# NSA score products in two single-pass fp32r matmuls, with a new order of the attention steps

## What is computed

```
kb   = rope(k_slc), kwin = rope(k_win)                 # (512, 2 groups, 64)
s    = einsum('q h d, k d -> h q k', qg, k) * scale     # 4 heads share a group's keys
p    = masked_softmax(s, key <= query)
o    = g_cmp * o_cmp + g_slc * (p_slc @ v_slc) + g_win * (p_win @ v_win)
```

## Time and profile before

| | |
|---|---|
| median of 3 runs | 1097.6 us (1094.86 to 1098.27) |
| the profiled execution | 1095.02 us, its span 1093.2 us |
| granted TensorE clock, mean | 0.996 |
| PE busy | 1073.5 us, 98% of the span |
| PE weight loads | 888.5 us, 81% |
| DVE, ACT, POOL busy | 608.3, 474.4, 481.4 us (56%, 43%, 44%) |
| DMA | 100.10 MB |
| NSA steps | from 754.3 us to about 963 us of the span |

### The profile page before, as it was taken

The page is one execution under the profiler, slowest core; times in us unless marked ns, Lnnn a source line. Parts: engine busy times, 40 slices in busy tenths (PEclk is TensorE's granted clock), DMA queues, the critical chain, the costliest instruction groups (busy, mean ns, idle before and its releaser), DMA issues. The chain is left out here.

```text
span 1093.2 us, 16412 instructions
## 1 busy us (share of the span) xinstructions
PE 1073.5 (98%) x5755; PEld 888.5 (81%) x5755; DVE 608.3 (56%) x1349; ACT 474.4 (43%) x1009; POOL 481.4 (44%) x276
## 2 busy tenths in 40 slices
PE   7999999999999999999999999999999999989996
PEld 6888888888888888888888888887788888767775
DVE  6667746766737556522122125436956765554667
ACT  6644356665543431431331233353334444454545
POOL 5785423232326775774675475356222122113230
PEclk9999999999999999999999999999999999999999
DMA  7554532211106354343442644604112012000011
GB/s 222 139 133 104 132 98 65 59 57 54 40 20 184 95 173 146 104 155 127 133 155 75 180 132 118 154 20 116 40 40 68 20 40 58 20 11 15 20 63 78
DMA packets 167158, 100.10 MB, mean 92 GB/s; under 512 B 30424, under 2 KB 160812, under 8 KB 166060
## 3 DMA queue, kind: packets, MB, share of 16 engines
q1 hardware_dynamic: 166924, 99.06, 31.4%
q10 hardware_dynamic: 160, 0.07, 0.0%
HBM read 95.69 MB, written 3.16 MB: 90 GB/s over the span
## 5 line engine op out<-in xcount | busy, mean ns | idle before, releaser
L1245 POOL TENSOR_TENSOR wlo<-stage,whi 128x1024 fp32r<-128x1024 f32 (+1 forms) x105 | 272.8, 2603 | 216.8 <-ACT whi L741 216.6
L2245 PE MATMUL ps<-hhi,whi 128*128 128x512 f32 (+1 forms) x728 | 311.8, 428 | 2.4 <-DVE gated L2007 1.9
L2245 PE MATMUL ps<-hhi,wlo 128*128 128x512 f32 (+1 forms) x728 | 294.3, 404 | 0.0
L2245 PE MATMUL ps<-hlo,whi 128*128 128x512 f32 (+1 forms) x728 | 285.4, 396 | 0.0
L2245 PEld LDWEIGHTS ps<-hhi,whi 128*128 128x128 f32 (+1 forms) x728 | 137.1, 188 | 37.1 <-issue 6.8
L741 ACT ACTIVATE whi<-stage 128x1024 fp32r<-128x1024 f32 x104 | 109.6, 1055 | 120.5 <-PE ps L2245 89.9
L2245 PEld LDWEIGHTS ps<-hhi,wlo 128*128 128x128 f32 (+1 forms) x728 | 137.3, 189 | 30.1 <-issue 6.3
L1343 POOL TENSOR_TENSOR wlo<-stage,whi 128x1024 fp32r<-128x1024 f32 (+3 forms) x40 | 73.4, 1837 | 190.9 <-ACT whi L1035 190.9
L2245 PEld LDWEIGHTS ps<-hlo,whi 128*128 128x128 f32 (+1 forms) x728 | 137.3, 189 | 24.2
L1123 ACT ACTIVATE prob<-ps,aneg 128x128 f32<-128x128 f32 (+1 forms) x96 | 50.7, 529 | 171.7 <-DVE aneg L2038 121.3
L2245 PE MATMUL ps<-ahi,whi 128*128 128x512 f32 x312 | 124.2, 398 | 0.0
(11 more groups left out here) (401 smaller groups left out, 1770.0 us busy)
## 6 DMA issues: line engine op xcount, KB each, us to landing
stage<-dn_w_in SPq DMA_DIRECT2D x32, 512.0 KB, 4.1
stage<-mlp_w_up SPq DMA_DIRECT2D x32, 512.0 KB, 4.9
stage<-mlp_w_down SPq DMA_DIRECT2D x32, 512.0 KB, 4.6
mod_w<-ada_w SPq DMA_DIRECT2D x8, 1536.0 KB, 6.5
stage<-w_in SPq DMA_DIRECT2D x17, 512.0 KB, 3.6
gcrow<-gc_rows SPq DMA_DIRECT2D x16, 256.0 KB, 3.5
stage<-dn_w_out SPq DMA_DIRECT2D x8, 512.0 KB, 3.7
stage<-w_in SPq DMA_DIRECT2D x9, 256.0 KB, 3.1
```

The source lines that it names most:

```text
L1245: pool.tensor_tensor(wlo[:, slot, 0:ks, 0:cols], stage[:, slot, 0:ks, 0:cols], whi[:, slot, 0:ks, 0:cols], ALU.subtract).then_inc(s["w_lo" ...
L2245: mm = pe.matmul(bank, w[:, slot, k - ks[0], 0:width], x[:, k], start=(i == 0), stop=(i == len(todo) - 1))
```

## The change

For each branch, the keys of one group are split in a high half (fp32r) and a low half (the rest). `kst[b][:, g]` holds the high half on the group's own 64 partitions, and the low half on the other 64. For each pair of steps a query tile is split too: `q_high` has the high half of one head's queries on both halves of the partitions, `q_low[g]` the low half on the group's partitions and zeros on the others. The score is then two fp32r matmuls into one bank: `q_high` by `kst` (high by high and high by low), `q_low` by `kst` (low by high). ACT writes the high halves (4 activations of 64x512 for the keys, 2 of 64x128 for each of 32 query tiles), and DVE the low ones (4 subtractions of 64x512, 32 of 64x128). Where the keys were rotated by two sums of 64x512, one of 128x512 does it, into scratch tiles. POOL zeroes two `q_low` buffers of 128x256 in place of two `kz` of 128x1024.

The order of the NSA steps becomes head, group, query tile, branch: both branches of a query tile follow each other, and share its split. The tile of steps i + 2 and i + 3 is split in step i, at ACT behind `turned(i - 2)`, at DVE as the first of `jobs(i)`. The MLA steps and all sums behind the scores stay. (Hunks with only a new semaphore name or an empty line are left out.)

```diff
@@ -249,7 +249,7 @@
         kT2_at = place[0]
-        kz = [sb("kz0", [P, 2, T]), None]
+        kst = [sb("kst0", [P, 2, T], F32R), None]
         v2 = [sb(f"v2_{b}", [P, CH, P]) for b in range(2)]
@@ -282,7 +282,8 @@
         gated = sb("gated", [P, 2, T])
-        kz[1] = at("kz1", [P, 2, T], F32, gated_at)
+        kst[1] = at("kst1", [P, 2, T], F32R, gated_at)
+        krot = [zth, prob[:, 1]]
         rcos = sb("rcos", [P, T])
@@ -308,7 +309,9 @@
         o_mla = at("o_mla", [P, CH, QW], F32, kT2_at)
-        csq = at("csq", [P, 3, T], F32, mlp_end + 5 * T * 4)
+        csq = at("csq", [P, 3, T], F32, mlp_end + T * 4)
+        q_low = [at(f"q_low{g}", [P, 2, P], F32R, mlp_end + (6 * T + g * 3 * P * 2) * 4) for g in range(2)]
+        q_high = at("q_high", [P, 2, P], F32R, mlp_end + 7 * T * 4)
 
@@ -477,11 +480,15 @@
             if i < N_NSA:
-                return "nsa", i // 16, i // 8 % 2, i // 4 % 2, i % 4
+                return "nsa", i // 16, i % 2, i // 8 % 2, i // 2 % 4
             return "mla", (i - N_NSA) // 4, None, None, i % 4
...
             return slice(g * DK, (g + 1) * DK)
+
+        def query_tile(n):
+
+            return n // 8, n // 4 % 2, n % 4
 
@@ -1085,15 +1092,33 @@
 
+            def key_high(b):
+                after(act, "dve", f"post {('ks', 'kw')[b]}")
+                for g in range(2):
+                    act.activation(kst[b][group(g), g], krot[b][group(g), :], ACT.Copy).then_inc(s["k_hi"], 1)
+
+            def query_high(n):
+                e, g, qt = query_tile(n)
+                after(act, "dve", f"post q{e}")
+                if n >= 2:
+                    act.wait_ge(s["at_s"], 2 * n - 2)
+                src = q2T[group(g), e, qt * P:(qt + 1) * P]
+                act.activation(q_high[group(g), n % 2], src, ACT.Copy)
+                act.activation(q_high[group(1 - g), n % 2], src, ACT.Copy).then_inc(s["qt_hi"], 1)
+
             taken("vs")
...
                 split_two(ahead_of(name))
+                if name == "gk":
+                    key_high(0)
                 if name == "kw":
...
                     done(act.activation(gate2[:, :, :], gate2[:, :, :], ACT.Tanh, scale=0.5), "gate tanh")
+                    query_high(0)
+            key_high(1)
 
@@ -1124,7 +1149,7 @@
             def turned(i):
-                keys = (i % 4 + 1) * P
+                keys = (step_key(i)[4] + 1) * P
                 act.wait_ge(s["at_t"], i + 1)
@@ -1198,6 +1223,8 @@
                     turned(i - 2)
+                if i % 2 == 0 and i + 2 < N_NSA:
+                    query_high(i // 2 + 1)
                 jobs(i)
@@ -1354,9 +1381,7 @@
             pool.memset(o_nsa[:, :, :], 0.0)
-            pool.memset(kz[1][:, :, :], 0.0)
-            pool.memset(minus_half[:, :], -0.5)
-            done(pool.memset(kz[0][:, :, :], 0.0), "zero")
+            done(pool.memset(minus_half[:, :], -0.5), "zero")
 
@@ -1371,12 +1396,16 @@
             for name in UNITS2[0:6]:
...
                     cosine("kr")
+                    after(pool, "dve", "norm low 6")
+                    pool.memset(q_low[0][:, :, :].bitcast(F32), 0.0).then_inc(s["qt_zero"], 1)
+                    pool.memset(q_low[1][:, :, :].bitcast(F32), 0.0).then_inc(s["qt_zero"], 1)
 
@@ -1876,9 +1905,7 @@
                     after(dve, "pool", "zero")
-                    for g in range(2):
-                        ins = dve.tensor_tensor(dst[group(g), g], rcos[group(g), :], rsin[group(g), :], ALU.add)
-                    done(ins, f"post {name}")
+                    done(dve.tensor_tensor(dst, rcos[:, :], rsin[:, :], ALU.add), f"post {name}")
                 else:
@@ -1886,8 +1913,20 @@
 
+            def key_low(b, g):
+                dve.wait_ge(s["k_hi"], 2 * b + g + 1)
+                dve.tensor_tensor(kst[b][group(1 - g), g], krot[b][group(g), :], kst[b][group(g), g], ALU.subtract).then_inc(s["k_lo"], 1)
+
+            def query_low(n):
+                e, g, qt = query_tile(n)
+                dve.wait_ge(s["qt_hi"], n + 1)
+                if n == 0:
+                    dve.wait_ge(s["qt_zero"], 2)
+                dve.tensor_tensor(q_low[g][group(g), n % 2], q2T[group(g), e, qt * P:(qt + 1) * P],
+                                  q_high[group(g), n % 2], ALU.subtract).then_inc(s["qt_lo"], 1)
+
             turned_rows(0, "vs")
-            rotated("ks", kz[0], None)
+            rotated("ks", krot[0][:, :], None)
             rotated("q0", q2T[:, 0], "ks")
@@ -1895,7 +1934,11 @@
             done(dve.tensor_scalar(gate2[:, :, :], gate2[:, :, :], 0.5, 0.5, ALU.mult, ALU.add), "gates")
-            rotated("kw", kz[1], "kr")
+            key_low(0, 0)
+            key_low(0, 1)
+            rotated("kw", krot[1][:, :], "kr")
+            query_low(0)
+            key_low(1, 0)
 
@@ -2025,7 +2068,7 @@
             def most(i):
-                qt = i % 4
+                qt = step_key(i)[4]
                 dve.wait_ge(s["at_s"], i + 1)
@@ -2072,8 +2115,11 @@
             def jobs(i):
+                if i % 2 == 0 and i + 2 < N_NSA:
+                    query_low(i // 2 + 1)
                 if i == 0:
                     turned_rows(1, "vw")
+                    key_low(1, 1)
                 if 3 <= i < 11:
@@ -3002,20 +3048,25 @@
                 if kind == "nsa":
-                    if qt == 0 and g == 0:
-                        after(pe, "dve", f"post {('ks', 'kw')[b]}")
-                        after(pe, "dve", f"post q{e}")
-                    q, k = q2T[:, e, qt * P:(qt + 1) * P], kz[b][:, g, 0:(qt + 1) * P]
+                    n = i // 2
+                    if e == 0 and qt == 0:
+                        pe.wait_ge(s["k_lo"], 2 * b + g + 1)
+                    if b == 0:
+                        pe.wait_ge(s["qt_hi"], n + 1)
+                        pe.wait_ge(s["qt_lo"], n + 1)
+                    keys = kst[b][:, g, 0:(qt + 1) * P]
+                    pe.matmul(bank[:, 0:(qt + 1) * P], q_high[:, n % 2], keys, start=True, stop=False)
+                    pe.matmul(bank[:, 0:(qt + 1) * P], q_low[g][:, n % 2], keys, start=False, stop=True).then_inc(s["at_s"], 1)
                 else:
...
                     q, k = qm[:, e % 4, qt * P:(qt + 1) * P], km[:, e % 4, 0:(qt + 1) * P]
-                pe.matmul(bank[:, 0:(qt + 1) * P], q, k, start=True, stop=True).then_inc(s["at_s"], 1)
+                    pe.matmul(bank[:, 0:(qt + 1) * P], q, k, start=True, stop=True).then_inc(s["at_s"], 1)
 
             def turned(i):
-                qt = i % 4
+                qt = step_key(i)[4]
                 pe.wait_ge(s["at_exp"], i + 1)
```

More of the change, by code:

```diff
@@ L356, in build @@
             kr_in mod_c mod_in mod_done c2_in pos_in cpos_in w2_in wv_in wq_in act_steps dve_steps pool_steps pe_steps
-            e_sq e_add at_s at_mask at_max at_neg at_exp at_t at_tev at_o at_inv at_coef at_done
+            e_sq e_add k_hi k_lo qt_zero qt_hi qt_lo at_s at_mask at_max at_neg at_exp at_t at_tev at_o at_inv at_coef at_done
             mlp_relu mlp_f mlp_hi mlp_lo grow_in inv_out1""".split():
```

## The result

| | before | after |
|---|---|---|
| median of six runs each | 1097.9 us (1094.9 to 1098.4) | 1110.2 us (1107.9 to 1111.1) |
| ratio, with its 95% interval | | 1.0115 [1.0103, 1.0128] |
| span of the profiled execution | 1093.2 us | 1108.0 us |
| its granted clock, mean | 0.996 | 0.985 |
| PE busy, instructions | 1073.5 us | 1073.8 us, x5755 |

A forecast was written before the change was run, and what follows sets the result against it. PE's own matmul stream was taken to bound the NSA stage. 15.7 - 5.3 - 2.3 - 0.7 = 7.4 us of gain gave 1087.6 from the profile, 1090.2 from the median; forecast 1088.5, range 1081 to 1095.

The forecast's parts named there:

- Products: NSA scores on PE: two fp32r matmuls in place of a float32 one gain 15.7 us (bounds 11.5 and 17.6).
- rival 1: NSA scores at 128 columns: narrow fp32r matmuls cost four passes, gain 11.5 instead of 15.7, 1092.7 us; chance 0.18.
- Opening: First NSA steps: wlo blocks query_low(0), PE stands 4.4 us, 0.9 more follows; loss 5.3 us (2.3 to 8).
- rival 4: Gap at the opening: PE's clock falls, costing 1.4 to 1.7 us, time 1090; chance 0.12.
- Step 34: Latent sums, through step 32's chain: query_low(17), blocked by wlo, makes PE wait; loss 2.3 us (0.3 to 3).
- The other tiles: Later NSA steps: scores(i + 2) waits 0.2 us for query_low in 8 of 16 cases; loss 0.7 us (0 to 4).
- Rival 3: At scores(i + 2) waiting on query_low, DVE behind POOL becomes the bound, slower than before, 1107 us; chance 0.08.

The follow-up runs named there:

- without most splits: Changed kernel with query tiles split only for the first two tiles, later steps using stale splits: 1104.9 us, ratio 1.0066.
- kept-busy run: Changed kernel plus idle-work PE matmuls, 16 ahead of scores(0) and 7 ahead of the first latent sums: 1100.4 us, ratio 1.0019.
- run with one product: Changed kernel with PE kept busy over both gaps (1100.4 us), without each NSA score's second product, query_low by keys: 1098.4 us, ratio 1.0012.
- square: ACT squares ckv ahead of the block exponentials at step 32, on the changed kernel with the opening reordered (1100.5 us): 1100.3 us, ratio 1.0035.
- ACT's two edits: Copy of step i - 2 ahead of exp of step i, query high halves one step sooner, on the reordered-opening, early-square kernel (1100.3 us): 1090.8 us.
- `x base`: DVE makes x base first in step 0, not in step 1, on the kernel with opening, square and ACT's copies early (1090.8 us): 1087.7 us.
- opening reordered: Changed kernel with query_high(0) right behind key_high(0), query_low(0) and key_low(0, 0) ahead of the gates, key_low(0, 1) behind: 1100.5 us, ratio 1.0042.
- ACT's edits only: Changed kernel with the copy of step i - 2 ahead of exp of step i and high halves one step sooner: 1101.3 us, ratio 1.0020.
- copy first alone: Copy of step i - 2 ahead of exp of step i, without earlier high halves, on the reordered-opening, early-square kernel (1100.3 us): 1100.1 us.

## Why the prediction was wrong

1. **Products.** Right in kind: one pass at every width, so rival 1 falls. The term was 15.7 and is 12.3: the changeover of two short matmuls with a weight load each costs more than the 0.03 I added (0.31 at 128 columns where 0.27 was forecast, 0.55 at 512 where 0.49). An estimate from the Trainium skill ("TensorE: Matmul & The Clock Gate", "Back-to-back issue gap"; about 81 ns for each) would have made the pair 0.16; the trace, with 0.31, disagrees.
2. **Opening.** The meeting with `wlo` came as worked out: PE's start 758.36, forecast 758.7. The term was 5.3, and step 2 started 8.8 us late, as the clock fell behind the gap. I had that as rival 4, but priced it at 1.4 to 1.7 us from the earlier trace rows, a mean over 5 us, without asking how long the low clock would last. It lasted 12 us. One number of the working is off as well: by its own prices the three narrower scores save 0.7 us up to step 2, not 0.9.
3. **Step 34.** Forecast 2.55 us of wait by ACT's `csq`, measured 1.73, but not by the path forecast: `wlo` blocked `acoef` and not `query_low(17)`, and the wait is 1.36 us with the new order alone and 1.54 without most splits. It is mostly the order's. And 4.9 us of clock stand behind it that I had not priced at all. Of the sum's losses these two clock terms are 10.8, shown by the kept-busy run (9.8).
4. **The other tiles: the step that failed as much as the clock.** "The unblocked 16 cost nothing: DVE has 62 us idle ... ACT's 64 small copies go where it waits for DVE". The idle time was there, but an in-order stream doesn't put new work into it: `query_low` waited for ACT 23 times, 18.9 us in all, with the next maximum behind it, and the exp behind that maximum, and the copy behind that exp, and PE behind the copy. The last link, the copy behind the exp, weighs most: the traces give 7.1 us for it and 3.3 for the wait for `q_high`. I looked for the cost where PE reads the new tile (0.7 us, though 0.2 us in 8 cases is 1.6 by itself); PE never waited for `q_low` beyond the opening, and only five later `q_low` rows exceed 0.4 us where I feared sixteen blocks. The cost, 9 to 10 us, sat at an old wait, whose slack went with the faster products (the run with one product puts 4.4 us more there) and with the new order.
5. **Order.** I priced the new order only by its opening. Alone it cost 3.8 us. They don't add to items 3 and 4: its waits are at the latent sums and at the transposes, too.

The sum forecast 7.4 us of gain and 12.3 were lost, 19.7 apart: 3.4 in the products, 9.8 by the clock (kept-busy run), 8.9 by ACT's order (that edit alone on the change) make 22.1, so they overlap a little.

Rival 3 named the right result, slower, and its 1107 us lie near 1110.2 by luck: about half of what was missing was the clock's, and DVE did not become the bound, since two edits in ACT's order gave 8.9 us back with all of DVE's work in place. Its place, scores(i + 2) on `query_low`, decides only when `query_low` is put behind the next maximum (13.0 us of waits, 4.3 of them the opening's).

From 1110.2 to 1087.7, in the order of the runs: opening (with the clock behind step 34) 9.7, square 0.2, ACT's two edits 9.6, `x base` 3.0.

## What to carry to other kernels

Idle time of an in-order engine is not by itself room for new work: follow the queue behind each new wait until it reaches the bounding engine, through the buffers that engines hand over to each other. When the bounding engine is made faster, look at the waits that were nearly zero before, for their slack is what the gain is taken from. Price a gap in a matmul stream by what the clock does behind it, and where the work can't be moved, fill the gap. When two kernels differ by a few us, compare executions of like granted clock, or an edit that pays can look worthless.

## What the hardware did that I had not expected

How long a gap is doesn't tell what the clock does. A wait of 1.69 us at the latent sums was followed by a clock of 1.00 in the kernel with the opening reordered, one of 2.09 us by half clock in the kernel with ACT's edits only:

```profile
874.91 0.58 PE L2859 MATMUL ps<-const,csq 128*128 128x1 f32 x4 [1.69 <-ACT csq L1185]
878.00:882.00 4.00, 3.83 (x26) 3.40 (x24) 3.03 (x9) 1.02 (x6) 0.00 (x0) 1.00 0.02 4
```

```profile
874.22 0.58 PE L2863 MATMUL ps<-const,csq 128*128 128x1 f32 x4 [2.09 <-ACT csq L1185]
878.00:882.00 4.00, 4.00 (x15) 3.52 (x15) 3.05 (x10) 0.50 (x2) 0.00 (x0) 0.50 0.00 0
```

In the changed kernel 1.73 us sufficed for a fall, and with the copy first alone 1.09 us in front of a transpose did (at 871.11; a clock of 0.82 from 870 to 874, then 0.50), while 1.45 us at the same transpose did not in the kernel without that edit. What decides between them these runs don't show. The Trainium skill ("TensorE: Matmul & The Clock Gate", "The HAM clock gate") says that an idle array goes back to half rate. The falls behind waits agree with that; it doesn't tell why the clock stayed at 1.00 behind the 1.69 us.
